# T forms of the down weights beside the units, and h turned out of the layer norm's rows in the third block

## The reference

```python
h = concat([meta, x])                                # 16 + 2048 tokens, width 1024
u = (h @ w_in) in 4 groups of 256 features
pooled = trailing mean of u over 2, 4, 8, 16 tokens  # one width per group
m = (group_linear(pooled - u) * scale) @ w_out
h = layer_norm(ALPHA * h + m, ln_mix_g, ln_mix_b)
gate, up = split(h @ ffn_w_gu)                       # 2816 features each
h = layer_norm(ALPHA * h + (silu(gate) * up) @ ffn_w_down, ln_ffn_g, ln_ffn_b)
return h[16:]
```

## Time and profile before

| what | before |
|---|---|
| median of 3 runs | 1759.36 us |
| the profiled execution | 1760.91 us |
| its span | 1759.1 us |
| TensorE busy | 1680.4 us, 96% |
| VectorE busy | 991.3 us, 56% |
| ScalarE busy | 580.5 us, 33% |
| GpSimd busy | 601.7 us, 34% |
| DMA | 307.75 MB, 175 GB/s on the mean |
| blocks 0, 1, 2, 3 end at | 136.5, 245.4, 342.2, 447.4 us |
| units | 449.9 to 1319.1 us |
| down | 1319.1 to 1748.4 us |

### The profile page before, as it was taken

The page is one execution under the profiler, slowest core; times in us unless marked ns, Lnnn a source line. Parts: engine busy times, 40 slices in busy tenths (PEclk is TensorE's granted clock), DMA queues, the critical chain, the costliest instruction groups (busy, mean ns, idle before and its releaser), DMA issues.

```text
span 1759.1 us, 18878 instructions
## 1 busy us (share of the span) xinstructions
PE 1680.4 (96%) x7400; PEld 1383.1 (79%) x7400; DVE 991.3 (56%) x1055; ACT 580.5 (33%) x790; POOL 601.7 (34%) x361
## 2 busy tenths in 40 slices
PE   7999888989699999999989999999998999999997
PEld 6887667877588888888868888888886888888786
DVE  6649669586764444434474444444453444459657
ACT  5232223233433333333353333333332432332220
POOL 0033342141533434443335666665542000242002
PEclk9999989999899999999999999999999999999999
DMA  8557665767443425435245454455548443555532
GB/s 320 215 207 243 222 252 194 255 239 246 167 143 120 138 75 174 147 114 171 92 148 151 132 154 145 136 170 175 188 122 292 166 141 135 203 200 192 175 137 100
DMA packets 172936, 307.75 MB, mean 175 GB/s; under 512 B 7088, under 2 KB 108592, under 8 KB 163120
## 3 DMA queue, kind: packets, MB, share of 16 engines
q1 hardware_dynamic: 172848, 306.54, 51.7%
HBM read 218.96 MB, written 87.56 MB: 174 GB/s over the span
## 4 chain that ended last, share of the span: by engine, by line
PE 78%; DVE 9%; DMA 8%; POOL 2%; ACT 2%; SPq 1%; issue 1%; ACTq 0%; DVEq 0%; POOLq 0%
PE acc L947 40%; PE acc L976 16%; PE turn L947 6%; PE acc L809 5%; PE turn L976 5%; PE acc L793 5%; DVE sums L1298 2%; DVE split L1265 2%; DMA raw<-w_in 1%; DMA h_dram<-z 1%; DMA nat_mix<-h_dram 1%; DMA dwr<-w_down 1%; DMA dt_raw<-w_down 1%; DMA raw<-w_out 1%; PE turn L781 1%
## 5 line engine op out<-in xcount | busy, mean ns | idle before, releaser
L947 PE MATMUL acc<-fa,wf 128*128 128x512 f32 x3168 | 733.0, 391 | 21.8 <-ACT acc L1194 12.5
L947 PEld LDWEIGHTS acc<-fa,wf 128*128 128x128 f32 x3168 | 595.9, 189 | 146.8 <-issue 20.0
L976 PE MATMUL acc<-dw,da 128*128 128x512 f32 x1386 | 318.4, 391 | 7.2 <-DVE da L1471 6.1
L976 PEld LDWEIGHTS acc<-dw,da 128*128 128x128 f32 x1386 | 260.9, 189 | 63.5 <-DVE da L1471 6.9
L1404 DVE TENSOR_TENSOR wf<-wt,wf 128x512 fp32r<-128x512 f32 x132 | 123.2, 934 | 190.7 <-ACT wf L1102 190.5
L1404 DVE TENSOR_TENSOR wf<-wr,wf 128x512 fp32r<-128x512 f32 x176 | 167.3, 958 | 82.7 <-ACT wf L1102 82.3
L809 PE MATMUL acc<-split,act_sb 128*128 128x512 f32 x768 | 181.6, 397 | 15.5 <-DVE split L1265 6.5
L793 PE MATMUL acc<-mov,split 128*128 128x512 f32 x768 | 184.1, 400 | 7.3 <-DVE split L1265 6.7
L644 POOL TENSOR_TENSOR wt<-wr,wt 128x512 f32<-128x512 f32 x88 | 130.1, 1479 | 163.2 <-DVE wf L1404 163.1
L809 PEld LDWEIGHTS acc<-split,act_sb 128*128 128x128 f32 x768 | 146.5, 192 | 48.7 <-DVE z L1320 7.2
L1102 ACT CAST wf<-wr 128x512 fp32r<-128x512 f32 x176 | 108.7, 618 | 223.6 <-PE acc L947 220.9
(11 more groups left out here) (96 smaller groups left out, 1383.3 us busy)
## 6 DMA issues: line engine op xcount, KB each, us to landing
wr<-w_gu SPq DMA_DIRECT2D x44, 1024.0 KB, 5.0
dar<-af_dram SPq DMA_DIRECT2D x56, 704.0 KB, 4.1
af_dram<-g SPq DMA_DIRECT2D x33, 512.0 KB, 3.4
raw<-w_in SPq DMA_DIRECT2D x16, 1024.0 KB, 8.7
raw<-fold_dram SPq DMA_DIRECT2D x16, 1024.0 KB, 6.9
fs<-hf_dram SPq DMA_DIRECT2D x14, 1024.0 KB, 7.5
dt_raw<-w_down SPq DMA_DIRECT2D x11, 1024.0 KB, 8.4
wt_dram<-dt_t SPq DMA_DIRECT2D x11, 1024.0 KB, 5.2
```

Of the source, the lines that this page charges most:

```text
L947: mm = nc.tensor.matmul(dst, wf[:, slot, a, k, :], fa[i][:, v, :, k, :], start=i < 2 and k == 0 and n3 == 0, stop=k == KC - 1 and n3 == 2, ...
L976: mm = nc.tensor.matmul(down_bank(k), da[k % 3][:, v, p, :], dw[:, slot, a, :], start=p == 0 and n3 == 0, stop=p == JF - 1 and n3 == 2)
```

## The change

- The T forms of the down weights leave the mixer blocks. They are made in 22 half steps (256 columns) in units 3 to 24, in buffers at the place of the layer norm's `gb`; the feed-forward's `gb` is loaded after them, in unit 27.
- Half 0's pairs: the rows of tokens 0 to 511 are loaded once, in block 1's outward phase, into a new buffer `h0` (2 MiB). In block 2 the turns read them and, for tokens 512 to 1023, the rows of z to which the layer norm has just been applied. Each turn waits for its row; `load_z(2)` waits for all turns. The turns of pairs 0 to 2 stand in hidden chunks 1 to 3, those of pair 3 between the row tiles of outward chunk 0. Copies, pair sums and stores move along.
- Half 0's forms: 0 and 1 are made in block 3's hidden phase, 2 and 3 and then 4 in its outward phase, 5 and 6 at places 1 and 2 of unit 0. `fs` has three buffers; the third lies at the place of `g`, so the first gate output waits for the forms.
- Half 1's forms: `fb0` has a place of its own and is made in unit 18, the others go one buffer down, so form i waits for product i - 1 of unit 21 in place of product i. Their places are spread over units 21 and 22, and their loads over three places of SyncE's list.
- Down: `load_da` leads by three steps in place of four, two rows of h are loaded ahead of the first step and one per step after that, rows 4 to 7 wait for the stored S forms. The first down weights wait one product longer.

The core of the diff (each "..." leaves out lines):

```diff
+        h0 = at("h0", R0 + 32 * KB, [P, TT, D])
         st_mix = at("st_mix", R0 + 48 * KB, [P, 4, KC, P])
+        ss_mix = at("ss_mix", R0 + 56 * KB, [P, 4, KC, P])
...
+        fa = [[at(f"fa{i}", R0 + FA_AT[i] * KB, [P, 2, TT, KC, P], F32R) for i in range(NP)]]
+        fa.append([at("fb0", Z0, [P, 2, TT, KC, P], F32R)])
+        fa[1] += [at(f"fb{i}", R0 + FA_AT[i - 1] * KB, [P, 2, TT, KC, P], F32R) for i in range(1, NP)]
+        fs = [at(f"fs{n}", off, [P, TT, KC, P]) for n, off in enumerate((N0, V0, G0))]
...
+        dt_raw = at("dt_raw", GB0, [P, 4, TOK // 2])
+        dt_t = at("dt_t", GB0 + 4 * KB, [P, 4, TOK // 2])
...
+        def pair_rows(pi, a):
+            if pi >= TT:
+                return nat[:, a]
+            return (h0 if a == 0 else z)[:, pi]
-        FS_SLOT = (0, 1, 0, 1, 0, 1, 0, 0, 1, 2, 3, 0, 1, 2)
+        FS_SLOT = (0, 1, 0, 1, 0, 1, 2, 0, 1, 0, 1, 0, 1, 0)
-        NEW_FORM_AT = [(HALF_UNITS - 1, place) for place in range(3, 7)] + [(HALF_UNITS, place) for place in range(3)]
+        NEW_FORM = {(0, 1): NP - 2, (0, 2): NP - 1, (HALF_UNITS - 4, 3): NP}
+        NEW_FORM.update({(HALF_UNITS - 1, place): NP + q for place, q in ((1, 1), (3, 2), (5, 3))})
+        NEW_FORM.update({(HALF_UNITS, place): NP + q for place, q in ((0, 4), (1, 5), (4, 6))})
+        TF0, TF_STEPS = 3, 2 * JF
...
             def load_z(s):
                 if s:
                     sp.wait_ge(rows_stored, s * (16 * TT))
+                if s == 2:
+                    sp.wait_ge(turn_done, TT * TT)
+            def w_down_cols(w, step):
+                half = slice(step % 2 * (TOK // 2), (step % 2 + 1) * (TOK // 2))
+                return w[:, :, step // 2, half].rearrange("b p n -> p b n")
+            def load_h0(j):
+                sp.dma_start(h0[:, j, :], h_rows[:, j, :]).then_inc(h0_landed[j], 16)
...
             def load_hz(m):
-                sp.wait_ge(prod_done, NP * UP_LAST + (6 if m < MT // 2 else 7))
+                if m < MT // 2:
+                    sp.wait_ge(prod_done, NP * UNITS)
+                else:
+                    sp.wait_ge(s_stored, 64 * JF)
...
+                if i >= 2:
+                    load_h0(2 * i - 4)
+                    load_h0(2 * i - 3)
+            for i in range(PAIRS):
+                load_chunk(c_in(2, i), i % 2, w_in[i])
+            load_chunk(c_mix(2, 0), 0, fold_dram[0])
+            store_h(1, 0)
+            load_x(3, 0)
+            load_chunk(c_mix(2, 1), 1, fold_dram[1])
             store_pair(0)
+            load_x(3, 1)
+            load_chunk(c_mix(2, 2), 0, fold_dram[2])
+            store_h(1, 1)
             store_pair(1)
+            load_x(3, 2)
+            store_h(1, 2)
+            load_chunk(c_mix(2, 3), 1, fold_dram[3])
             store_pair(2)
+            store_h(1, 3)
+            load_z(2)
+            load_x(3, 3)
+            load_chunk(c_in(3, 0), 0, w_in[0])
             store_pair(3)
+            load_chunk(c_in(3, 1), 1, w_in[1])
+            load_chunk(c_in(3, 2), 0, w_in[2])
             load_form(0)
             load_form(1)
+            load_chunk(c_in(3, 3), 1, w_in[3])
+            store_h(2, 0)
+            load_chunk(c_mix(3, 0), 0, fold_dram[0])
             load_form(2)
+            load_chunk(c_mix(3, 1), 1, fold_dram[1])
             load_form(3)
+            store_h(2, 1)
+            store_h(2, 2)
+            load_chunk(c_mix(3, 2), 0, fold_dram[2])
+            store_h(2, 3)
+            load_z(3)
+            load_form(6)
+            load_form(4)
+            load_chunk(c_mix(3, 3), 1, fold_dram[3])
+            load_form(5)
             load_unit(0)
             load_unit(1)
...
+                if TF0 <= n <= TF0 + TF_STEPS:
+                    if n > TF0:
+                        store_tform(n - TF0 - 1)
+                    if n < TF0 + TF_STEPS:
+                        load_tform(n - TF0)
...
                 if n == TURN0 + 3 * TT:
+                    load_form(NP)
+                    load_form(NP + 1)
+                if n == HALF_UNITS - 3:
+                    load_form(NP + 2)
                 if n == HALF_UNITS - 1:
+                    load_form(NP + 3)
                     load_form(NP + 4)
                     load_form(NP + 5)
+                if n == HALF_UNITS:
                     load_form(NP + 6)
...
             load_da(2)
+            load_hz(0)
+            load_hz(1)
             for k in range(DSTEPS):
...
+                if k + 3 < DSTEPS:
+                    load_da(k + 3)
+                if k + 2 < MT:
+                    load_hz(k + 2)
...
+                if TF0 <= n < TF0 + TF_STEPS:
+                    tform(n - TF0)
...
             if v < 16:
-                eng.wait_ge(prod_done, NP * UP_LAST + 1 + v // 4)
+                eng.wait_ge(prod_done, NP * UP_LAST + 2 + v // 4)
...
+                    if b == 2 and i >= 2:
+                        take_turn(i - 2, 2)
+                        take_turn(i - 2, 3)
                     if i >= 1:
                         d_hi(b, i - 1)
+                    if b == 2 and i >= 1:
+                        take_turn(i - 1, 0)
+                        take_turn(i - 1, 1)
+                    if b == LAST and i >= 2:
+                        form_hi(i - 2)
...
                     if b < LAST:
                         x_hi(b + 1, i)
+                        if b == 2 and i == 0:
                             for k in range(KC):
+                                take_turn(TT - 1, k)
```

More of the change, by code:

```diff
@@ L153, in trunk @@
         rows_stored = sem("rows_stored")
+        h0_landed = [sem(f"h0_landed{n}") for n in range(4)]
         tf_landed = sem("tf_landed")
@@ L158, in trunk @@
         ss_stored = sem("ss_stored")
-        fs_landed = [sem(f"fs_landed{n}") for n in range(4)]
+        fs_landed = [sem(f"fs_landed{n}") for n in range(3)]
         wr_landed = [sem("wr_landed0"), sem("wr_landed1")]
@@ L607, in _ @@
                 load_dw(0, q)
-            for m in range(MT // 2):
-                load_hz(m)
             load_da(2)
-            for m in range(MT // 2, MT):
-                load_hz(m)
-            load_da(3)
+            load_hz(0)
+            load_hz(1)
             for k in range(DSTEPS):
@@ L946, in product @@
                     for n3, (a, v) in enumerate(PARTS):
[L947 removed]
+                        mm = nc.tensor.matmul(dst, wf[:, slot, a, k, :], fa[half][i][:, v, :, k, :],
                                               start=i < 2 and k == 0 and n3 == 0, stop=k == KC - 1 and n3 == 2,
@@ L1077, in form_hi @@
                 act.wait_ge(fs_landed[FS_SLOT[q]], 16 * (fs_uses(q) + 1))
-                if half:
-                    act.wait_ge(prod_done, NP * (HALF_UNITS - 1) + i + 1)
+                if half and i:
+                    act.wait_ge(prod_done, NP * (HALF_UNITS - 1) + i)
+                elif half:
+                    act.wait_ge(st_stored, 16 * 2 * TT)
+                    act.wait_ge(ss_stored, 16 * 2 * TT)
                 elif i < 2:
@@ L1088, in form_hi @@
                     act.wait_ge(chunk_done, MIX_END)
-                nc.scalar.copy(fa[i][:, 0], fs[FS_SLOT[q]][:]).then_inc(fa_hi, 1)
+                nc.scalar.copy(fa[half][i][:, 0], fs[FS_SLOT[q]][:]).then_inc(fa_hi, 1)
             def unit_hi(n, i):
@@ L1429, in mixer_block @@
                             apply(b - 1, j)
+                    if b == LAST and i >= 2:
+                        form_lo(i - 2)
                 for i in range(PAIRS):
```

198 lines of the change are left out of this document (73 added, 125 removed).

## The result

The changed kernel takes **1749.12 us** (median of 5 runs, 1747.41 to 1751.27) beside 1759.32 us for the kernel before (5 runs, 1756.16 to 1760.26): a ratio of 0.9942, 95% interval 0.9931 to 0.9953. That is faster by 10 us, where 39 were forecast, and outside the predicted range of 1703 to 1744. The profiled execution took 1751.27 us with a span of 1749.5.

What follows compares the result with a forecast made beforehand. TensorE's work was taken as nearly constant per stage, with 81 us of waiting to close. Terms -17.5 + 4.7 - 10.2 - 11 + 0 + 1 - 6 = -39.0 on a span of 1759.1 gave 1720 us, range 1703 to 1744.

Steps and rivals of the forecast that it cites:

- Block 2, +4.7: Block 2 takes in turns, copies and pair sums and goes from 96.8 to 101.5 us; bounds -3 to +13.
- The prediction's own sign of being wrong: The prediction counts as wrong if block 2 or the middle costs over 10 us more, or units grow over half a microsecond.
- 6 + 3: In block 2, 6 us for the 16 turns and 3 us for the lower granted clock, on 87.5 of work.
- Rival 2: Block 2 inherits block 3's trouble (+13) and block 3 keeps its z wait (-3): 1743 us; chance 0.19.
- Block 1, -17.5: Without T forms, block 1's hidden phase falls by 6.7 us and its outward phase by 10.8.
- The term of -10.8: Block 1's outward phase falls from 58.4 to 47.6 us: the z wait goes and the last chunk's queue shortens.
- Block 3, -10.2: Block 3 loses turns, pair loads and pair sums and goes from 107.7 to 97.5 us; bounds -17 and 0.
- Start of the units, -11: With forms 5 and 6 behind the bank copy, gap and clock loss of 12.9 + 2.3 become 4; bounds -14 and -5.
- Middle, 0: At the change of halves, 1.5 + 5 of gap and 2 of clock, so no change; bounds -8 and +4.
- T forms beside the units, +1: T forms made in units 3 to 24 cost 1 us, their GpSimd work being nearly hidden; bounds 0 and +6.
- Rival 3: T forms hold VectorE, making bank C's sum late in units; 57 us go on the path: 1777 us; chance 0.05.
- Down, -6: Fewer h rows ahead and earlier weight issue cut waiting at down's start from 8.3 to 2 us; bounds -8 and 0.

Runs made afterwards that it cites:

- e1: Changed kernel with a second buffer for the turned copies of odd pairs, with its own semaphore: 1727.76 us, ratio 0.9825.
- e2: Changed kernel, one buffer, with block 2's pair stores ahead of chunk and x loads in SyncE's order: 1727.55 us, ratio 0.9817.
- e10: Changed kernel with e1, e2, e6, e7 and e9 joined, z(2) asked for earlier, forms 5 and 6 both at place 3 of unit 0: 1701.84 us.
- e11: Kernel before, T form transfers and waits kept, but GpSimd sums only 8 of 512 columns from the second step on: 1737.93 us, ratio 0.9878.
- e12: Kernel before, all T form sums kept, but their transfers carry only 8 of 512 columns from the second step on: 1752.52 us, ratio 0.9962.
- e4: Kernel before without any T forms, the down stage reading w_down blocks in their place: 1731.73 us, ratio 0.9839.
- e9: Changed kernel with block 3's last fold chunk loaded ahead of z and forms 6 and 4: 1746.47 us, ratio 0.9919.
- e7: Changed kernel, half 1's form 6 loaded ahead of unit 22's T form transfers, half 0's form 6 made at place 3 of unit 0: 1741.61 us.
- e3: Changed kernel without any T forms, the down stage reading down weight blocks in their place: 1742.12 us, ratio 0.9910.
- e5: Kernel before with only the T forms moved out of the mixer blocks to units 3 to 24: 1731.56 us, ratio 0.9844.
- e6: Changed kernel with down's last activation and S form stores issued after step 1's loads: 1741.42 us, ratio 0.9891.

## Why the prediction was wrong, point by point

**Block 2, +4.7 and really +30.0: the step that failed.** The prediction costed the copies as work ("16 copies on ScalarE") and asked of each turn whether its layer norm row, its copy's place on ScalarE, and z were in time. It never asked when the copy's destination would be free: that wait was put at nothing. The list of the change says that "Copies, pair sums and stores move along"; with them moves the wait for the one buffer, and the store that ends it stands where SyncE's order puts it, not where the pair is done. 22 of the 25 us of error are this wait (e1, e2). That a waiting instruction holds back all behind it was known and was applied to chunks and to z, not to the four stores. The numbers were at hand: the earlier trace rows has 8.0 us for a landing, and the pace of pairs is a chunk, 10.94 us. Fetching, turning, summing and storing a pair through one buffer in 10.94 us leaves no room for a store that waits 8 us for its turn. The prediction's own sign of being wrong, block 2 over 10 more than before, is what came.

The rest of the term was nearly right. Without the wait the block takes 104.4 where 101.5 was laid out. z(2) was taken at 2 and was 6.5. In e10, gaps of 3.6 over 87.5 of work leave 7.8 for turns and clock, against 6 + 3. Rival 2 had the right doubt, one queue in order, but in the wrong places: z and the fold chunk, at +13 together.

**Block 1, -17.5 and -21.3.** Right in kind. The hidden phase came out at 43.5 for 43.8 forecast, and VectorE's pooling operations at 1.22 to 1.25. In the outward phase the split that was to be 1.8 late was 0.56 late, and z was there 67.4 after the block's start for 68.5 forecast. The term of -10.8 was -14. e11 and e12 correct the reason: the prediction put it on z and on the queue alone, and of the outward phase's 58.7 us, taking the long sums away gives 9 back (e11), taking the transfers away 10 (e12), both 15 (e4).

**Block 3, -10.2 and -11.6.** The gap named ahead of the last outward chunk is the one that is there, 5.15 for 6 forecast, and e9 shows its cause (the chunk's place behind z and two forms) and what the prediction did not see: the forms and the units' first weights need that place too.

**Start of the units, -11.** The gap ahead of product 4 is 3.53, for 3 forecast, ended by the seed of bank C behind form 6 on VectorE, and e7 removes it by that edit.

**Middle, 0.** 1.39 + 6.62 against 1.5 + 5 forecast. The larger one ends with form 6 of half 1, which SyncE issues behind T form transfers (e3: 2.55 without them; e7: 3.27 with the load ahead of them).

**T forms beside the units, +1.** e4 and e5 differ by 0.2 us. Rival 3 (57 us) is out: TensorE is busy 380.00 of the 380 us from 490 to 870 in after as in before. VectorE's operations stretch there too (178.02 us busy in this window in e5, 174.49 in e4), but the slack takes it. The sums were priced too low, at 0.65 each: in after 72 of them take 61.0 us of GpSimd in this window, 0.85 each, and that is hidden as well.

**Down, -6 and really +1.8: the second step that failed**, with 8 us. The activation form that was late is in time now, as forecast: a gap of 1.92 that before has there is gone. TensorE so comes to the next weights 30.1 us after the stage's start in place of 32.3. The weights are not earlier: they are still issued behind the last a and s stores, 26.5 us after the start where before has 26.6. TensorE waits there for what it has gained and 0.7 more (7.05 for 4.14), and the 66 matmuls behind that gap take 17.79 for 16.88. On SyncE's timeline of after:

```profile
1327.22 1.00 SPq L470 DMA_DIRECT2D af_dram<-sx  x2
1328.26 2.87 SPq L470 DMA_DIRECT2D af_dram<-sa  x2
...
1334.19 1.29 SPq L486 DMA_DIRECT2D dwr<-w_down  x2
```

The stores wait for GpSimd's last S forms, and two of those lengthen, beside VectorE's work on activation forms. These two of the four in after, and the first's counterpart in before, where all four last 2.39:

```profile
1317.20 3.79 POOL L683 TENSOR_TENSOR sx<-sa,g 128x1024 f32<-128x1024 f32 x1
...
1323.54 3.66 POOL L683 TENSOR_TENSOR sa<-sa 128x1024 f32<-128x1024 f32 x1
```

```profile
1327.30 2.39 POOL L644 TENSOR_TENSOR sx<-sa,g 128x1024 f32<-128x1024 f32 x1
```

The prediction removed the loads ahead of the weights from its list and forgot to ask what the stores in the same list wait for. e6 gives the 9.8 us.

**The sum.** -21.3 + 30.0 - 11.6 - 8.4 + 1.8 = -9.5, on a span that fell by 9.6. With block 2 at the 104.4 of e1 and e2 the same sum comes to 1727.7, what those two measured, and with e6's order of down as well to 1718, near the 1720 forecast (worked out; the two were not run together without other edits). The size rested on two queue positions that were not looked at, and the first of them is most of it. That the rest then meets the forecast so closely is in part luck: blocks 1 and 3 gained 5.2 more than forecast and down with e6's order 2 more, and block 2 without its wait lost 3.2 more and the units gained 1.6 less.

## What to carry to other kernels

When operations are moved nearer together, ask of each one not only whether its input is ready but when its output's place is free: who empties it, where that store stands in its queue, and what each issue ahead of it waits for. A write-back is as urgent as a load when a single buffer stands behind it. And try the parts of a change by themselves: here one part gave 28 us and the rest took 17.6 back, where one wait in the rest cost 22.

## What the runs showed of the hardware

GpSimd's sums, not the traffic, were what slowed VectorE in the hidden phases: 305 GB/s beside it changed nothing (e11), 29 us of sums did (e12). The same is seen in after where pair sums run in block 2, first on VectorE (a split is 2.29 and a pooling operation 1.22 when alone), then on GpSimd (1.28 when alone):

```profile
272.41 2.36 DVE L1345 SCALAR_TENSOR_TENSOR sums<-stage,sums 128x1024 f32<-128x1024 f32 x1
274.69 3.38 DVE L1309 TENSOR_TENSOR split<-raw,split 128x2048 fp32r<-128x2048 f32 x1
```

```profile
275.88 3.35 POOL L683 TENSOR_TENSOR ss_mix<-ss_mix,st_mix 128x512 f32<-128x512 f32 x1
```

Both engines wait for each other, each by about one operation of the other. The Trainium skill (SBUF — State Buffer, Who interferes with whom) calls the shared port pair an exclusive lock for a whole instruction and says that DMA does not contend with an engine; the first agrees with these rows and with e12, the second with e11.

The three stores of 0.75 MiB from `st_mix` took 8.14, 9.02 and 10.39 us from issue to landing. The DMA shares of block 2's halves, 0.45 and 0.60, hide that the engines were nearly full just then. The windows of the three landings:

```profile
259.35:267.50 8.15, 0.51 (x3) 0.09 (x1) 4.32 (x3) 0.00 (x0) 0.76 (x1) 0.84 0.87 279
278.95:287.97 9.02, 3.80 (x17) 2.81 (x15) 4.87 (x3) 0.00 (x0) 2.43 (x2) 0.85 0.93 311
301.99:312.38 10.39, 0.00 (x0) 0.00 (x0) 0.00 (x0) 0.00 (x0) 0.00 (x0) 0.68 0.99 345
```

Each store was issued at most 0.9 us behind a chunk of 1 MiB, and the pair's sums, 1 MiB more, at most 2.6 us behind it. So each store went out among other transfers. How long it takes alone no run here shows.
